# One decoder layer on one core: weight slices on GpSimd, a ring of four PSUM banks, stores waited for a stage later

## The chip, the cores and the metric

The kernel runs on one NeuronCore of a Trainium2 chip, as one program of several stages. The metric is the device time in microseconds (us) of one launch, as the median of several runs. The core has a matmul engine (TensorE, PE in the profile), a vector engine (VectorE, DVE), a scalar engine (ScalarE, ACT), GpSimd (POOL) and SyncE (SP), which only issues DMAs. The engines run apart from each other and meet at semaphores, and at a barrier at the end of every stage.

## The reference, cut to what matters

One layer of a decoder works on 1,024 prompt tokens and on 8 sequences of 4 new tokens each, width 1,024, all in float32. The parts that the change touches:

```python
# after the input projection (h @ w_in) gives qa, ka, va, c_q, ckv, kpe, ga, gb
qb = rms_norm(c_q, g_q) @ w_uq                 # queries of the latent branch
k_nope = einsum('nsc,che->nshe', ckv, w_uk)    # prompt: keys and values from the latents
v      = einsum('nsc,che->nshe', ckv, w_uv)
# new tokens: attention over the cached, paged latents (1,024 past rows per sequence)
q_lat = einsum('nthe,che->nthc', q_nope, w_uk)
s = (q_lat . ckv_ext + q_pe . kpe_ext) * scale
o = (softmax(s) . ckv_ext) . w_uv
# branch A: dilated window attention; then gates, w_o, MLP and a gated embedding
```

A product of float32 matrices is made from three matmuls: each operand is split into a high and a low part, and high x high, high x low and low x high are summed.

## The kernel before, in words

`build` calls the stages in turn. Each is one `nc.Block()`: a separate instruction list for every engine, ended by a barrier of all engines. The order of the work on an engine is the order written out in its function; nothing else plans it.

**`project_natural`** (span 0 to 261 us) projects the tokens to queries, keys, values and latents in rows of tokens. Its last steps run on ScalarE: `take(s)` (L497 to L512) copies a PSUM bank to `nat` and issues two stores, to the scratch `q_d`, `k_d` or `v_d` (L505) and to an output (L512). At its end ScalarE waits until all stores have landed (L546, L547), and only then goes to the barrier.

**`project_gates`** (261 to 509 us) multiplies the activations by 16 slices ("units") of 128 columns of the gate weights, three chunks of 352 tokens each (`multiply_chunk`, L639 to L641). GpSimd splits each unit's weights into high and low (`split_weights`, L2293 and L2295), and TensorE waits for the split of unit m before its first chunk. The first two units are split in the stage before. Between chunks, `samples_at(n)` places the pieces of the cached window attention of 8 sequences. TensorE does `turn_new` after the second chunk: it transposes the new queries and keys (`q_new`, `k_new`, L814) that SyncE has loaded from the scratch. SyncE's list is in this order: the cached keys of sequence 0 into a ring (`load_keys(0)`: four DMAs of 64 KB, L1796, and one of 1 MB, L1797), `q_new` (L773), `k_new` (L774), the cached values of sequence 0 (`load_values(0)`, five such DMAs), mask, new values, `load_keys(1)`, 14 loads of latent weights (`load_latent_weights`), and then the gate weights of units 2 and 3 (`load_unit`, L758). ScalarE stores a unit's gates (L973) and at the end waits for those stores (L979).

**`project_latents`** (509 to about 600 us) runs over nine groups of up to 128 tokens. In step t TensorE transposes latents (`turn_latents`, L1093 to L1102), multiplies the queries (`queries`, L1120 to L1122) and transposes them (`turn_queries`, L1138). VectorE does `scale_latents(t+1)` (L1263), `take_keys(t+1)` (L1273, L1274, L1277), then waits for ScalarE's query copies and does `rotate_queries(t)`, six operations on SBUF (L1288 to L1295). ScalarE makes high parts and copies the queries. GpSimd makes the low parts `cq_lo` (L1067) and `ckv_lo` (L1072), clears half of `kb_t` in step 0 (L1076), and in steps 2 and 4 splits the two weight arrays `w_uk` and `w_uv` whole: L1081 (high) and L1083 (low), 128x1024 each. They are needed only after the nine steps. Before the steps VectorE does `scale_latents(0)`, the three low parts of `w_uq` (L1302) and `take_keys(0)`.

**`attend_latent`** follows, and then **`attend_latent_sample`** (759 to 824 us), the attention over the cached latents, in two batches of four sequences. For each sequence TensorE transposes eight page tiles of 2 x 128 columns in four groups, and one rotary group (`turn_keys`, L1878 and L1881). Group n goes to PSUM bank 3 + n % 2, and is copied out by ScalarE (even n, L1967) or VectorE (odd n, L1838 and L1840); group n waits for the copy of group n - 2. The order on TensorE is: keys of sequences 0 to 3, `scores(0)` (L1897 to L1909), keys 4 and 5, `turn_probs(0)` (L1919, to banks 5 and 6), keys 6, `values(0)` (L1932, L1934), keys 7, `turn_result(0)`, `scores(1)`, `turn_probs(1)`, `values(1)`, `turn_result(1)`, and the products with `w_uv`. After the scores VectorE finds the largest (L1997) and ScalarE takes the exponential (L1971), and each of them is written ahead of that engine's copies of keys 4. SyncE loads the cached rows of sequences 3 to 7 in this stage (`load_rest`, L1764), eight DMAs each.

Window attention (`attend_window`) and the tail (merge, MLP, embedding; `run_tail`) are as before.

## Time and profile before

| | |
|---|---|
| runs | 2025.71, 2026.61, 2032.1 us; median 2026.61 |
| the profiled execution's own time | 2029.21 us |
| its span | 2027.5 us |
| TensorE matmul busy | 1912.4 us, 94% |
| TensorE weight load busy | 1760.7 us, 87% |
| VectorE, ScalarE, GpSimd busy | 795.1, 498.5, 754.1 us |
| mean granted TensorE clock | 0.974 of full speed |

Times in the profile are counted from the start of the span. A row of a timeline gives the start, the time taken, the engine, the line, the operation, output<-input, shapes and count, and in brackets how long the engine had been idle before it and what ended that. PEclk 1.00 is TensorE's 2.4 GHz, 0.50 its 1.2 GHz.

### The profile page before, as it was taken

The page shows a single profiled execution, that of the slowest core. Times are in us where ns is not written, and L with a number is a line of the kernel's source. Part 1 is how long each engine was busy: PE and PEld are TensorE (multiplying, and loading weights), DVE is VectorE, ACT ScalarE, POOL GpSimd, SP SyncE. Part 2 cuts the span into 40 slices and gives each one's busy share as a digit, 9 for nine tenths or more (in the row PEclk, how much of TensorE's full clock was granted, in tenths as well). Part 3 has the DMA queues.
Part 4 walks back from the last instruction along what each step waited for, and adds up shares of the span by engine and source line. Part 5 has one row for each costly group of instructions (what it writes and reads, how often), then busy time and mean ns, then how long its engine had stood idle before and what let it go on. Part 6 is the DMA issues. An engine that isn't in the chain of part 4 may idle for free.

```text
span 2027.5 us, 35016 instructions
## 1 busy us (share of the span) xinstructions
PE 1912.4 (94%) x13421; PEld 1760.7 (87%) x13421; DVE 795.1 (39%) x1752; ACT 498.5 (25%) x1052; POOL 754.1 (37%) x519
## 2 busy tenths in 40 slices
PE   6899979999799988798999999999999999999898
PEld 6887779998666665677999999999999999999897
DVE  4244212222636663475445531123112212255565
ACT  4232112232446552363112110001001000122222
POOL 4312112321404101100666565355436534566421
PEclk9999989999799999799999999999999999999999
DMA  6333374551002005503431331232133113311202
GB/s 215 97 104 109 125 219 148 184 178 61 10 23 68 6 1 181 136 2 129 142 102 42 115 134 52 83 125 93 45 131 126 52 42 125 134 42 42 81 24 86
DMA packets 184508, 193.40 MB, mean 95 GB/s; under 512 B 16314, under 2 KB 157466, under 8 KB 183618
## 3 DMA queue, kind: packets, MB, share of 16 engines
q1 hardware_dynamic: 167138, 161.85, 24.9%
q10 hardware_dynamic: 14816, 28.12, 4.0%
q0 software_dynamic: 2432, 1.74, 0.3%
q8 instruction: 84, 1.38, 0.3%
q14 instruction: 38, 0.31, 0.0%
HBM read 161.13 MB, written 63.97 MB: 111 GB/s over the span
## 4 chain that ended last, share of the span: by engine, by line
PE 49%; DVE 1%; DMA 1%; issue 1%; ACT 1%; POOL 0%; DVEq 0%; ACTq 0%; POOLq 0%
PE bank L639 16%; PE bank L640 16%; PE bank L641 16%; DMA f_gates<-gate_d 1%; DVE x_res L2372 0%; PE bank L2439 0%; PE bank L2400 0%; DVE f_diag L2457 0%; PE bank L2402 0%; PE bank L2401 0%; DMA out_y_prompt<-y_nat 0%; PE bank L2476 0%; PE bank L2429 0%; DVE f_hg L2370 0%; ACT tail_square L2247 0%
## 5 line engine op out<-in xcount | busy, mean ns | idle before, releaser
L639 PE MATMUL bank<-h_hi,wu_hi_tail 128*128 128x352 f32 x960 | 310.9, 324 | 3.4 <-POOL wu_lo_tail L2295 3.4
L640 PE MATMUL bank<-h_lo,wu_hi_tail 128*128 128x352 f32 x960 | 308.4, 321 | 0.0
L641 PE MATMUL bank<-h_hi,wu_lo_tail 128*128 128x352 f32 x960 | 308.4, 321 | 0.0
L2293 POOL TENSOR_TENSOR wu_hi_tail<-w_stage_tail,ones 128x1024 fp32r<-128x1024 f32 x88 | 168.4, 1914 | 273.2 <-PE bank L641 161.8
L639 PE MATMUL bank<-a_hi,wu_hi_tail 128*128 128x352 f32 x768 | 247.7, 323 | 0.0
L640 PE MATMUL bank<-a_lo,wu_hi_tail 128*128 128x352 f32 x768 | 246.1, 320 | 0.0
L641 PE MATMUL bank<-a_hi,wu_lo_tail 128*128 128x352 f32 x768 | 245.9, 320 | 0.0
L2295 POOL TENSOR_TENSOR wu_lo_tail<-w_stage_tail,wu_hi_tail 128x1024 fp32r<-128x1024 f32 x88 | 219.6, 2495 | 6.9
L2250 ACT ACTIVATE a_hi<-f_hg 128x352 f32 x96 | 47.8, 498 | 603.0 <-DVE f_hg L2356 603.0
L639 PEld LDWEIGHTS bank<-h_hi,wu_hi_tail 128*128 128x128 f32 x960 | 180.6, 188 | 3.7 <-issue 3.7
L2339 DVE TENSOR_TENSOR x_res<-bank,x_res 128x352 f32 x120 | 63.0, 525 | 301.4 <-PE bank L641 301.2
L640 PEld LDWEIGHTS bank<-h_lo,wu_hi_tail 128*128 128x128 f32 x960 | 180.9, 188 | 0.0
L641 PEld LDWEIGHTS bank<-h_hi,wu_lo_tail 128*128 128x128 f32 x960 | 180.8, 188 | 0.0
L2305 POOL TENSOR_TENSOR a_lo<-f_hg,a_hi 128x352 f32 (+1 forms) x96 | 91.1, 950 | 144.9 <-ACT a_hi L2250 144.9
L640 PEld LDWEIGHTS bank<-a_lo,wu_hi_tail 128*128 128x128 f32 x768 | 144.3, 188 | 0.0
L639 PEld LDWEIGHTS bank<-a_hi,wu_hi_tail 128*128 128x128 f32 x768 | 144.1, 188 | 0.0
L641 PEld LDWEIGHTS bank<-a_hi,wu_lo_tail 128*128 128x128 f32 x768 | 143.9, 187 | 0.0
L2353 DVE TENSOR_TENSOR f_tmp<-bank,rstd_bc 128x352 f32<-128x352 f32 x96 | 50.3, 524 | 233.2 <-PE bank L641 233.0
L639 PE MATMUL bank<-h_hi,wu_hi_gates 128*128 128x352 f32 x384 | 129.3, 337 | 10.6 <-POOL wu_lo_gates L2295 6.8
L436 PE MATMUL bank<-wn_hi,h_hi 128*128 128x512 f32 (+5 forms) x360 | 133.6, 371 | 0.0
L438 PE MATMUL bank<-wn_hi,h_lo 128*128 128x512 f32 (+5 forms) x360 | 131.6, 365 | 0.0
L437 PE MATMUL bank<-wn_lo,h_hi 128*128 128x512 f32 (+5 forms) x360 | 131.2, 364 | 0.0
(332 smaller groups left out, 3759.0 us busy)
## 6 DMA issues: line engine op xcount, KB each, us to landing
w_stage_tail<-in_w_up SPq DMA_DIRECT2D x32, 512.0 KB, 4.0
w_stage_tail<-in_w_down SPq DMA_DIRECT2D x32, 512.0 KB, 3.8
gate_d<-gate_out ACTq DMA_DIRECT2D x16, 528.0 KB, 3.4
f_gates<-gate_d ACTq DMA_DIRECT2D x24, 352.0 KB, 3.2
w_stage_gates<-in_w_in SPq DMA_DIRECT2D x16, 512.0 KB, 6.8
ws_ring<-in_cache_win_k SPq DMA_DIRECT2D x8, 1024.0 KB, 5.7
ws_ring<-in_cache_win_v SPq DMA_DIRECT2D x8, 1024.0 KB, 6.6
ls_keys<-in_cache_ckv SPq DMA_DIRECT2D x64, 128.0 KB, 2.2
```

Of the source, the lines that this page charges most:

```text
L436: pe.matmul(out, a, w, start=k == 0, stop=False)
L437: pe.matmul(out, a, v, start=False, stop=False)
L438: last = pe.matmul(out, c, w, start=False, stop=k == KD - 1)
L639: pe.matmul(out, w, a, start=n == 0, stop=False)
L640: pe.matmul(out, w, b, start=False, stop=False)
L641: last = pe.matmul(out, v, a, start=False, stop=n == len(ks) - 1)
L2250: act.activation(chunk_of(st.out[0], i, q), g.hg[:, q % 2:q % 2 + 1, :], ACT.Copy).then_inc(g.hi_s, 1)
L2293: pool.tensor_tensor(g.wu_hi[:, j], g.w_stage[:, j], one, ALU.mult).then_inc(g.w_hi, 1)
L2295: pool.tensor_tensor(g.wu_lo[:, j], g.w_stage[:, j], g.wu_hi[:, j].bitcast(F32), ALU.subtract).then_inc(g.w_split, 1)
L2305: pool.tensor_tensor(chunk_of(st.out[1], i, q), g.hg[:, q % 2:q % 2 + 1, :], chunk_of(st.out[0], i, q).bitcast(F32), ALU.subtract).then_in ...
L2339: dve.tensor_tensor(x, g.bank[:, q:q + 1, :CH], x, ALU.add).then_inc(g.free, 1)
L2353: dve.tensor_tensor(g.tmp[:, q % 2, :], g.bank[:, q, :CH], g.rstd_bc[:, c * CH:(c + 1) * CH], ALU.mult).then_inc(g.free, 1)
```

## The change

Four edits, in four stages:

1. ScalarE no longer waits for the last stores at the end of `project_natural`. Those who read or overwrite what is stored wait in `project_gates`: SyncE before the loads of `q_new` and `k_new`, and ScalarE and VectorE before their first copies of turned cached keys. `load_values(0)` now stands ahead of these two loads.
2. In the same way the stores of the gates are waited for in `project_latents`: by GpSimd before its clearing of `kb_t`, and by VectorE before `take_keys(0)`, which now comes after the first of the three low parts of `w_uq`, ahead of the other two.
3. The split of `w_uk` and `w_uv` goes in eight slices of 128x256, one in each of the steps 0 to 7.
4. The cached latent attention turns into a ring of four banks (3 to 6), group n into bank 3 + n % 4, waiting for the copy of group n - 4. The probabilities' transposes take two places of the same ring (groups 30, 31 and 42, 43), and the keys of sequences 6 and 7 are numbered after them.

```diff
@@ project_natural
-            for j in range(3):
-                act.wait_ge(nat_out[j], written(len(stored), j))
@@ project_gates
+    def wait_stored(eng):
+
+        for j in range(3):
+            eng.wait_ge(g.nat_out[j], g.nat_stored[j])
+
     def take_turned(copy, eng, s, qs, odd):
...
+            if n < 2:
+                wait_stored(eng)
             eng.wait_ge(turned, n + 1)
...
             load_keys(0)
+            load_values(0)
+            wait_stored(sp)
             sp.dma_start(q_new[:, :], g.q_d[SEQ:, :]).then_inc(new_in, 16)
             sp.dma_start(k_new[:, :], g.k_d[SEQ:, :]).then_inc(new_in, 16)
-            load_values(0)
             sp.wait_ge(clear, 1)
...
-            for j in range(2):
-                act.wait_ge(gate_out[j], 16 * (units // 2))
@@ project_latents
                 if t == 0:
+                    for j in range(2):
+                        pool.wait_ge(g.gate_out[j], g.gates_stored)
                     odd_heads = g.kb_t[:RD].rearrange("p (a two) c -> p a two c", two=2)[:, :, 1, :]
                     pool.memset(odd_heads, 0.0).then_inc(clear, 1)
                     pool.wait_ge(l_in, LATENT_LOADS)
-                if t in (2, 4):
-                    hi, lo, w = ((uk_hi, uk_lo, g.w_uk_sb), (uv_hi, uv_lo, g.w_uv_sb))[t // 2 - 1]
-                    one = g.ones[:, 0:1].unsqueeze(2).to_broadcast([P, 2, H * E])
-                    pool.tensor_tensor(hi[:, :, :], w[:, :, :], one, ALU.mult).then_inc(w_hi_s, 1)
-                    pool.wait_ge(w_hi_s, t // 2)
-                    pool.tensor_tensor(lo[:, :, :], w[:, :, :], hi[:, :, :].bitcast(F32), ALU.subtract).then_inc(w_lo_s, 1)
+                if t < NT - 1:
+                    hi, lo, w = ((uk_hi, uk_lo, g.w_uk_sb), (uv_hi, uv_lo, g.w_uv_sb))[t // 4]
+                    part = (slice(None), t // 2 % 2, slice(t % 2 * 256, t % 2 * 256 + 256))
+                    pool.tensor_tensor(hi[part], w[part], g.ones[:, 0:1].to_broadcast([P, 256]), ALU.mult).then_inc(w_hi_s, 1)
+                    pool.wait_ge(w_hi_s, t + 1)
+                    pool.tensor_tensor(lo[part], w[part], hi[part].bitcast(F32), ALU.subtract).then_inc(w_lo_s, 1)
...
             scale_latents(0)
-            for k in range(3):
-                dve.wait_ge(uq_hi_s, k + 1)
-                dve.tensor_tensor(uq_lo[:, k, :], g.w_uq_sb[:, k, :], uq_hi[:, k, :].bitcast(F32), ALU.subtract).then_inc(uq_lo_s, 1)
+            low_query_weights(0)
+            for j in range(2):
+                dve.wait_ge(g.gate_out[j], g.gates_stored)
             take_keys(0)
+            low_query_weights(1)
+            low_query_weights(2)
@@ attend_latent_sample
+    base = [groups * s + (2 if s >= 6 else 0) for s in range(NSEQ)]
+    probs_at = [6 * groups, NSEQ * groups + 2]
+    ring = lambda n: 3 + n % 4
...
-                    if n >= 2:
-                        pe.wait_ge(k_got[n % 2], n // 2)
+                    if n >= 4:
+                        pe.wait_ge(k_got[n % 2], n // 2 - 1)
...
             def turn_probs(b):
                 pe.wait_ge(e_done, b + 1)
...
+                for half in range(2):
+                    n = probs_at[b] + half
+                    pe.wait_ge(k_got[n % 2], n // 2 - 1)
+                    for a in range(4):
+                        at = (4 * half + a) * P
+                        last = pe.transpose(g.bank[:, ring(n), a * P:(a + 1) * P], prob[:, at:at + P], g.ident[:, :])
+                    last.then_inc(k_full, 1)
```

## Rows read from the trace of the kernel before

**Rows 1.** PE's waits, whole span: line, releaser, us in total, times, longest us

```profile
PE bank L1138 <- DVE q_nat L1295: 7.0, 3, 2.8
```

**Rows 2.** Timeline, 250 to 272 us, the change from `project_natural` to `project_gates`

```profile
258.27 0.70 ACTq L512 DMA_DIRECT2D out_win_v_sample<-nat  x1
...
260.90 0.55 PE L639 MATMUL bank<-h_hi,wu_hi_gates 128*128 128x352 f32 x1 [3.74 <-PEq L310]
```

**Rows 3.** Lines L547 and L979: duration ns min/median/max, first and last start us

```profile
L547 ACTq EVENT_SEMAPHORE  x1: 38/38/38, 260.4 to 260.4; - x1
...
L979 ACTq EVENT_SEMAPHORE  x1: 17/17/17, 508.5 to 508.5; - x1
```

**Rows 4.** DMA issues at 262.62, 263.09 and 265.96 us: count, KB, us to landing

```profile
ws_ring<-in_cache_win_k SPq DMA_DIRECT2D x1, 1024.0 KB, 5.7
...
ws_q_new<-q_d SPq DMA_DIRECT2D x1, 64.0 KB, 5.2
...
ws_ring<-in_cache_win_v SPq DMA_DIRECT2D x1, 1024.0 KB, 8.6
```

**Rows 5.** Timeline, 268 to 300 us, up to the first wait for split weights

```profile
270.37 0.43 PE L814 MATMUL bank<-ident,ws_q_new 32*128 32x32 f32 x4
...
291.19 1.89 POOL L2293 TENSOR_TENSOR wu_hi_gates<-w_stage_gates,ones 128x1024 fp32r<-128x1024 f32 x1 [28.80 <-DMA w_stage_gates<-in_w_in]
...
295.56 0.66 PE L639 MATMUL bank<-h_hi,wu_hi_gates 128*128 128x352 f32 x1 [6.83 <-POOL wu_lo_gates L2295]
```

**Rows 6.** Table by stretches: length, busy by engine, then PEclk, DMA share, GB/s

```profile
298.00:299.00 1.00, 1.00 (x6) 1.00 (x6) 0.00 (x0) 0.00 (x0) 1.00 (x1) 0.73 0.77 229
```

**Rows 7.** Timeline, 505 to 515 us, the change from `project_gates` to `project_latents`

```profile
505.83 0.34 ACTq L973 DMA_DIRECT2D gate_d<-gate_out  x1
...
509.36 0.87 PE L1093 MATMUL bank<-ident,cq 128*128 128x128 f32 x3 [4.54 <-PEq L751]
...
512.22 2.08 DVE L1302 TENSOR_TENSOR uq_lo<-w_uq_sb,uq_hi 128x768 fp32r<-128x768 f32 x2 [0.46 <-ACT uq_hi L1199]
```

**Rows 8.** Timelines of DVE and POOL in `project_latents`, 538 to 554 us

```profile
538.82 0.55 DVE L1263 TENSOR_TENSOR cq_x<-bank,g_q_sb 128x384 f32<-128x384 f32 x1
...
542.96 1.53 DVE L1288 TENSOR_TENSOR lat_ra<-q_nat,cos_b_sb 128x128 f32<-128x128 f32 x1 [1.73 <-ACT q_nat L1244]
...
544.62 2.43 DVE L1290 TENSOR_TENSOR lat_rb<-q_nat,sin_b_sb 128x128 f32<-128x128 f32 x1
...
547.82 0.55 DVE L1263 TENSOR_TENSOR cq_x<-bank,g_q_sb 128x384 f32<-128x384 f32 x1
...
553.42 0.55 DVE L1263 TENSOR_TENSOR cq_x<-bank,g_q_sb 128x384 f32<-128x384 f32 x1
...
541.75 0.74 POOL L1072 TENSOR_TENSOR ckv_lo<-ckv_t,ckv_hi 128x256 fp32r<-128x256 f32 x1 [0.74 <-ACT ckv_hi L1212]
542.45 1.90 POOL L1081 TENSOR_TENSOR uv_hi<-w_uv_sb,ones 128x1024 fp32r<-128x1024 f32 x1
544.42 2.48 POOL L1083 TENSOR_TENSOR uv_lo<-w_uv_sb,uv_hi 128x1024 fp32r<-128x1024 f32 x1
```

**Rows 9.** Timeline of `attend_latent_sample`, 759 to 824 us

```profile
763.90 1.06 PE L1878 MATMUL bank<-ident,ls_keys 128*128 128x128 f32 x8 [0.50 <-DVE ls_key_t L1838]
...
780.36 1.23 DVE L1997 CUSTOM_DVE_ANT_0 ls_prob<-bank,ls_mask 128x1028 f32<-128x1028 f32 x1 [5.94 <-PE bank L1909]
...
783.41 1.97 PE L1878 MATMUL bank<-ident,ls_keys 128*128 128x128 f32 x8 [2.21 <-ACT ls_key_t L1967]
...
794.42 3.66 PE L1932 MATMUL bank<-ls_keys,ls_prob_t 128*32 128x256 f32 x64
...
802.52 1.92 PE L1897 MATMUL bank<-ls_key_t,ql_t 128*32 128x512 f32 x16 [0.34 <-issue]
```

**Rows 10.** Line L1764, issues of 759.0 to 763.7 us: count, duration ns, starts

```profile
L1764 SPq DMA_DIRECT2D ls_keys<-in_cache_ckv x9: 332/333/347, 759.4 to 763.6; - x9
...
DMA to landing us min/median/max: 2.0/2.3/5.4
```

More of the change, by code:

```diff
@@ L292, in project_natural @@
         g.sem, ("wn_in", "wn_hi", "wn_lo", "n_full", "n_got", "roped", "tabs", "ra_s"))
-    nat_out = [g.sem(f"nat_out{j}") for j in range(3)]
+    nat_out = g.nat_out = [g.sem(f"nat_out{j}") for j in range(3)]
     g.w_stage = Room(nc, g.gate_stage_at)("w_stage_gates", [P, 2, KD, P])
@@ L303, in written @@
         return 16 * sum(1 if stored[n][0] == 2 else 2 for n in range(place, m, 3))
+    g.nat_stored = [written(len(stored), j) for j in range(3)]
     def low_block(eng, b):
@@ L713, in project_gates @@
     gate_ready = g.sem("gt_ready")
-    gate_out = [g.sem(f"gt_out{j}") for j in range(2)]
+    gate_out = g.gate_out = [g.sem(f"gt_out{j}") for j in range(2)]
     ring_in = [sem(f"ring_in{j}") for j in range(3)]
@@ L1831, in take_keys @@
         for q in range(groups):
-            n = s * groups + q
+            n = base[s] + q
             if n % 2 != odd:
@@ L1840, in take_keys, with take_probs @@
                 copy(rope_t[:, s % BATCH, :, :].rearrange("p a c -> p (a c)"), src[:, :2 * P]).then_inc(k_got[odd], 1)
+    def take_probs(copy, eng, b, odd):
+        half = (odd - probs_at[b]) % 2
+        n = probs_at[b] + half
+        eng.wait_ge(k_full, n + 1)
+        if b >= 1:
+            eng.wait_ge(o_full, b)
+        copy(prob_t[:, 4 * half:4 * half + 4, :].rearrange("p a b -> p (a b)"), g.bank[:, ring(n), :]).then_inc(k_got[odd], 1)
     with nc.Block() as block:
@@ L1866, in turn_keys @@
                 for q in range(groups):
-                    n = s * groups + q
+                    n = base[s] + q
                     if q == 0:
@@ L1957, in _ @@
             pe.wait_ge(ot_got, 2)
+            for odd in range(2):
+                pe.wait_ge(k_got[odd], done(probs_at[1] + 2, odd))
             for h in range(H):
@@ L1984, in _ @@
             take_keys(copy, act, 5, 0)
-            take_probs(0)
+            take_probs(copy, act, 0, 0)
             take_keys(copy, act, 6, 0)
@@ L1988, in _ @@
             exponent(1)
-            take_probs(1)
+            take_probs(copy, act, 1, 0)
         @block.vector
```

57 lines of the change are left out of this document (25 added, 32 removed).

## The prediction

> **What bounds the kernel now.** The table of the profile says that TensorE is busy for 94% of the span, so time can only come from its idle stretches and from stretches at its lower clock. I read its waits first, then the timelines around the places that the change touches. The longest wait inside a stage is for the rotated queries [rows 1]. Three more places matter.
>
> At the first stage change TensorE is idle for 3.74 us up to 260.90 [rows 2]. ScalarE's last issue ends at 258.97 [rows 2], its wait for that store ends at 260.44 [rows 3], and 0.46 us later the next stage runs. At the second change the last issue ends at 506.17 [rows 7], the wait at 508.5 [rows 3], and the stage starts at 509.36 after 4.54 us of idling [rows 7]: 0.84 us after the wait.
>
> In `project_latents` VectorE sets the pace. From one L1263 to the next it takes 5.60 us without a weight split (547.82 to 553.42) and 9.00 us with one (538.82 to 547.82) [rows 8]. The 3.40 us are two rotations: L1288 lasts 1.53 us and ends 0.14 us after GpSimd's high part, L1290 lasts 2.43 us and ends 0.15 us after the low part [rows 8]. L1289 between them is not held.
>
> In the cached latent attention TensorE transposes two groups (eight transposes, 1.06 us) and then waits for a copy (0.50 us [rows 9], elsewhere down to 0.35): some 1.44 us for two groups. Without the waits, and as the last transpose's tail lies beside the next, it would be 0.92, or 0.46 us a group. After the scores both copying engines are taken by the softmax, TensorE runs dry for 2.21 us until 783.41, and then eight transposes take 1.97 us [rows 9]: the 1.2 GHz level.
>
> **The change, part by part.**
>
> *First stores waited later: 2.7 us.* The next stage starts 0.46 us after 258.97, at 259.43, so 1.47 us earlier. But `q_new` and `k_new` now stand behind the cached values. Before, the queries were issued at 263.09 and landed 5.2 us later [rows 4], at the very time at which the megabyte of keys ahead of them landed (262.62 + 5.7), and the megabyte of values landed 8.6 us after 265.96 [rows 4], 13.7 us into the stage. So this queue's data come one after the other, and the two small loads will land 12.5 to 13.7 us into the stage; I take 13.2, that is 272.6. TensorE needs them 9.5 us in (270.37 [rows 5]): a new stall of about 4 us, after which it stands 2.3 us later than before, and at the lower clock for a time, which costs another 1 to 2.5 us. What is late next is nothing: TensorE used to arrive at the third unit at 288.73 and to wait 6.83 us for its split [rows 5]. It now arrives 18.4 us after 272.6 plus the clock, at 292 to 293.5. The split hangs on SyncE's issues, whose order from the mask on is the same, and its data, GpSimd's 28.80 us of idling ending with them [rows 5]; it is ready 1.47 us earlier, at about 294.1. Cover for the stall is gone if the arrival goes beyond that. With the wait shrunk from 6.8 to about 1 us the clock should stay up: after 295.56 it was at 1.2 GHz until about 298.5 (0.73 in the slice from 298 [rows 6]), half of 3.0 us lost; I count 1.2 of these 1.5. Sum 1.47 + 1.2 = 2.7; bounds -0.5 (arrival past the split) and 3.2. SyncE's own wait costs nothing: it comes 4.5 us into the stage, the stores land 1.0 us into it. The waits of ScalarE and VectorE come after the fourth chunk, later still. `load_values(1)`, which waits for transposes before the third unit, is issued about 3.5 us later, but its values are used over 25 us after that.
>
> *Gate stores waited later: 2.3 us.* The stage starts 0.84 us after 506.17, at 507.0 instead of 509.36. VectorE comes to its new wait about 2.4 us in, at 509.4, GpSimd 5.4 us in, after the 508.5 at which the stores had landed: no cost. Bounds 2.0 and 2.7 (the 0.46 us of the first change).
>
> *Start of the latents: 1.2 us.* `take_keys(0)` moves ahead of two low parts (2.08 us for both [rows 7]), and TensorE's step 1 and the first queries with it: 2.2 us. GpSimd gives back 1.0: its first slice stands ahead of `cq_lo` of step 1, so that `cq_lo`, `ckv_lo` and the second slice all fall on the first rotation. Bounds 0 and 2.2.
>
> *Slices: 4.5 us.* A 128x256 subtraction takes 0.74 us, a 128x1024 one 2.48 [rows 8]: 0.58 us per 256 columns and 0.16 fixed. The 1.90 us of the high part [rows 8] give 0.16 + 1.74 / 4 = 0.60. In a step's time, with 542.45 as the start: high part to 543.05, low part 543.12 to 543.86. VectorE comes with L1288 at 542.96, as before, is held for 0.1 us (hidden by its own latency), passes L1289, and L1290 ends at 543.86 + 0.15 = 544.01 instead of 543.65: 0.37 us a step. Six steps (2 to 7) cost 2.2 us in place of 2 x 3.40 = 6.8: 4.6, say 4.5. Bounds: no hold at all (6.8), and a hold for the whole of both slices, 1.34 us a step (-1.2). I take the working by the rows since it follows the order seen there. The weights' last slice ends in step 7, before the products that need them.
>
> The Trainium skill, SBUF — State Buffer, "Who interferes with whom", says that VectorE with two SBUF inputs and GpSimd exclude each other for a whole instruction and that the one issued first has the port. The row agrees (2.43 us beside a 2.48 us one). Taken at its worst, a rotation held by every slice, the slices would cost more than the two whole arrays; that is a rival below.
>
> *Ring of four: 10.2 us.* The first stretch runs at 1.2 GHz until 763 and is TensorE's own; no gain. From then on a sequence (four groups and a half) takes 2.1 us instead of 3.3. Sequences 1 and 2 end at 767.5. SyncE issues nine loads of pages from 759.4 to 763.6, so sequence 3's eighth at 763.0, and the longest of them takes 5.4 us to land [rows 10]: 768.5, one us of waiting. The scores start at 771.2 instead of 774.5: 3.3 us. From there to L1997 (780.36) and to the copy that released 783.41 [rows 9] nothing changes: 3.05 us. But TensorE has four groups to do in it instead of two, idles for 1.4 us instead of 2.2, and has only rotary 4, sequence 5, the probabilities (together 3.3), sequence 6 (2.1), `values(0)` (3.66 [rows 9], with its small end 4.2), sequence 7 (2.1) and 0.8 of result and last copy left, all at full clock: 12.5 us. So `scores(1)` follows 3.05 + 12.5 = 15.5 us, say 15.3, after L1997 starts; before it was 802.52 - 780.36 = 22.2 [rows 9]: 6.9 us. Together 10.2. Nothing changes behind it. Bounds: 6.8 if the clock falls in the 1.4 us wait as it did before (from 783.2 to 790 at half rate, 3.4 us), and 13.4 if it stays up after the second softmax, too.
>
> **Sum**: 2.7 + 2.3 + 1.2 + 4.5 + 10.2 = 20.9 us. The profiled execution took 2029.2 (span 2027.5 and 1.7 around it), so 2008.3; it stands 2.6 us above the median of the runs, which gives 2005.7, and I predict 2006 for the median.
>
> **The rivals** (times as medians).
> - *The clock falls in the softmax wait.* For it: a 2.21 us gap was followed by 1.97 us for eight transposes [rows 9]. Against it: the gap is now 1.4 us with work on both sides. 17.5 us, 2009. Chance 0.20. The mirror case, one stretch of low clock less elsewhere, gives 2002.5: 0.10.
> - *The late queries are not absorbed.* They land beyond 14 us or the clock stays low for longer, so that TensorE reaches the third unit after its split. The first term falls to -0.5: 2009. Chance 0.10; the wait of 6.83 [rows 5] speaks against it.
> - *The slices hold the rotations for their full length.* 1.34 x 6 = 8.0 in place of 6.8: the slices' term is -1.2, in sum 15.2, 2011.5. L1289, which passed between two GpSimd operations [rows 8], speaks against it. Chance 0.07. It is what the skill's rule on the shared port gives at its worst.
> - *The ring doesn't run ahead*, because pages arrive late: at the pace of [rows 10] the 40 loads are issued by 781 and landed by 784; the last sequence is needed at 790. Only sequence 3 should wait; if each of the later ones waits 1 us, 2010. Chance 0.02.
> - *Slower than before.* In the ring the bursts and pauses of TensorE leave the clock at 1.2 GHz over the whole cached stage. It has some 44 us of work at full rate; each us of it at half rate costs one. It decides once 27 us more of this work than I count are at the lower level: all 44 would give 2029 to 2040. Against it: with the pauses of the old order the level was 2.4 GHz for most of the stage. Chance 0.02.
>
> **How the numbers follow.** My forecast has the remaining 0.49. Its own range, from clock alignment and the unknown port order, is 2002 to 2010. With the rivals the range is 2000 to 2015. A measurement here can tell 0.3% (6 us) from no change: faster by more than that 0.95 (all cases but the slow one and a pile-up of two or three of the others), within it 0.03, slower 0.02.
>
> **What would show it.** First gate stage: L814 waits for DMA about 4 us, then the wait for L2295 is about 1 us instead of 6.8. The second stage starts near 259.4, the third 1.2 us after the start of the last store's issue. L1263 to L1263 near 6.0 us in steps 2 to 7, no more 9.0, L1288 and L1290 under 1 us. In the cached stage no wait for key copies except at the softmax (about 1.4 us), scores 11.9 us after the stage's start (before 15.2), and eight transposes near 1.0 us afterwards. It is wrong if L1263's period is above 6.6, if TensorE is ready after the third unit's split, or if the cached stage is shortened by less than 7 us.

## The result, and the profile after

The changed kernel takes 2012.42 us, the median of four runs (2007.71 to 2014.73), beside 2028.15 for the kernel before on the same chip: a ratio of 0.991, with a 95% interval of 0.9894 to 0.9925 (the ratios here are estimated from all the runs; the two medians alone would give 0.992). The forecast was 2006, in a range of 2000 to 2015. So the sign and the range held, and about a quarter of the 20.9 us I had summed up did not come: the profiled executions are 2029.2 us before and 2013.7 after, 15.5 us apart.

I followed the gain from place to place. Each number is the start of the same instruction before less its start after:

| place | before | after | gained so far |
|---|---|---|---|
| first gate product | 260.90 | 259.60 | 1.30 |
| first transpose of the latents | 509.36 | 505.47 | 3.89 |
| third scaling of the latents | 524.21 | 519.30 | 4.91 |
| ninth scaling | 564.63 | 556.37 | 8.26 |
| first key product behind them | 573.69 | 565.27 | 8.42 |
| first transpose of the cached stage | 759.33 | 752.25 | 7.08 |
| its first scores | 774.53 | 766.50 | 8.03 |
| its second scores | 802.52 | 787.57 | 14.95 |
| first transpose of the next stage | 824.16 | 809.85 | 14.31 |

TensorE's timeline of the kernel after, in the gates' stage (start us, duration, engine and line; in brackets the idle time before it and what ended it), and under it GpSimd's:

```profile
259.60 0.40 PE L639 MATMUL bank<-h_hi,wu_hi_gates 128*128 128x352 f32 x1 [2.60 <-PEq L312]
...
273.78 0.63 PE L822 MATMUL bank<-ident,ws_q_new 32*128 32x32 f32 x4 [4.75 <-DMA ws_k_new<-k_d]
...
295.42 0.43 PE L639 MATMUL bank<-h_hi,wu_hi_gates 128*128 128x352 f32 x1 [1.49 <-POOL wu_lo_gates L2318]
...
291.04 1.90 POOL L2316 TENSOR_TENSOR wu_hi_gates<-w_stage_gates,ones 128x1024 fp32r<-128x1024 f32 x1 [29.95 <-DMA w_stage_gates<-in_w_in]
```

The reader is to see that the wait of 6.83 us for the split [rows 5] has become two: 4.75 us for the new keys, which TensorE takes up at 273.78 where the forecast had them landed at 272.6, and 1.49 us for the split. But TensorE goes on at 295.42 where it went on at 295.56 before: the third unit's weights arrive at 291.0 as before [rows 5], although the stage began 1.3 us earlier. ("Arrive" is the start of GpSimd's split, which ends its wait for them.) The table by stretches (length, busy time of PE, PEld, DVE, ACT and POOL, granted clock as a share of 2.4 GHz, DMA share, GB/s) shows what the second wait was worth. Of the kernel after:

```profile
270.00:275.00 5.00, 1.22 (x9) 1.16 (x10) 0.12 (x1) 0.13 (x1) 0.00 (x0) 0.61 1.04 263
275.00:280.00 5.00, 5.00 (x24) 5.00 (x25) 0.75 (x3) 0.00 (x0) 0.00 (x0) 0.71 0.75 176
...
295.00:300.00 5.00, 4.58 (x32) 4.06 (x36) 0.85 (x2) 0.60 (x1) 4.61 (x3) 1.00 0.90 282
```

and of the kernel before:

```profile
295.00:300.00 5.00, 4.44 (x19) 4.45 (x20) 0.00 (x0) 0.00 (x0) 4.73 (x3) 0.65 0.62 184
```

Before, TensorE came out of the wait at the lower level and ran 19 of the recorded products up to 300; now it comes out at 2.4 GHz and runs 32. The low clock has moved into the stretches from 270 to 280 (0.61 and 0.71), where the time it costs would have been waited away at 293.9 in any case.

In the latents, VectorE's and GpSimd's timelines of one step after:

```profile
519.30 0.55 DVE L1276 TENSOR_TENSOR cq_x<-bank,g_q_sb 128x384 f32<-128x384 f32 x1
...
523.44 0.29 DVE L1301 TENSOR_TENSOR lat_ra<-q_nat,cos_b_sb 128x128 f32<-128x128 f32 x1 [1.73 <-ACT q_nat L1253]
523.65 0.87 DVE L1302 TENSOR_TENSOR lat_ra<-q_nat,cos_b_sb 128x128 f32<-128x128 f32 x1
524.44 0.28 DVE L1303 TENSOR_TENSOR lat_rb<-q_nat,sin_b_sb 128x128 f32<-128x128 f32 x1
...
525.49 0.55 DVE L1276 TENSOR_TENSOR cq_x<-bank,g_q_sb 128x384 f32<-128x384 f32 x1
...
522.93 0.62 POOL L1090 TENSOR_TENSOR uk_hi<-w_uk_sb,ones 128x256 fp32r<-128x256 f32 x1
523.63 0.74 POOL L1092 TENSOR_TENSOR uk_lo<-w_uk_sb,uk_hi 128x256 fp32r<-128x256 f32 x1
```

The steps of 9.00 us are gone [rows 8]; each of the steps from the third scaling to the ninth takes 6.15 to 6.19 us now. One operation of a rotation, L1302, is held: it ends at 524.52, 0.15 us after GpSimd's low part, as the held ones did before. In one step it went the other way:

```profile
536.02 0.29 DVE L1302 TENSOR_TENSOR lat_ra<-q_nat,cos_b_sb 128x128 f32<-128x128 f32 x1
536.22 0.83 DVE L1303 TENSOR_TENSOR lat_rb<-q_nat,sin_b_sb 128x128 f32<-128x128 f32 x1
...
536.00 0.90 POOL L1092 TENSOR_TENSOR uv_lo<-w_uv_sb,uv_hi 128x256 fp32r<-128x256 f32 x1
```

Here L1302 keeps its 0.29 us, GpSimd's low part takes 0.90 us in place of 0.74, and L1303 is the one held.

The cached stage after:

```profile
752.25 3.57 PE L1906 MATMUL bank<-ident,ls_keys 128*128 128x128 f32 x16 [1.21 <-PEq L1366]
...
757.88 1.91 PE L1906 MATMUL bank<-ident,ls_keys 128*128 128x128 f32 x16
...
762.18 3.32 PE L1906 MATMUL bank<-ident,ls_keys 128*128 128x128 f32 x16 [2.18 <-DMA ls_keys<-in_cache_ckv]
...
766.50 1.92 PE L1924 MATMUL bank<-ls_key_t,ql_t 128*32 128x512 f32 x16 [0.56 <-ACT ls_key_t L1997]
...
775.38 0.44 PE L1909 MATMUL bank<-ident,ls_rope 128*128 128x128 f32 x2 [1.33 <-ACT ls_key_t L1997]
...
787.57 1.92 PE L1924 MATMUL bank<-ls_key_t,ql_t 128*32 128x512 f32 x16 [0.34 <-ACT ls_key_t L1997]
...
772.33 1.23 DVE L2021 CUSTOM_DVE_ANT_0 ls_prob<-bank,ls_mask 128x1028 f32<-128x1028 f32 x1 [5.94 <-PE bank L1936]
```

Sixteen transposes (four groups) in one run of 1.91 us where pairs of groups used to take 1.06 us and then wait [rows 9]: the four banks keep TensorE free of the copies. What it meets instead is sequence 3's pages, for 2.18 us, and behind that wait sixteen transposes take 3.32 us: the granted clock was 0.50 from 763 to 766.

### The profile page after: what moved, and what is told of

The parts are those of the page before. It is cut to its first block, busy times and chain, and to the rows that moved or that the text cites. A ratio compares the mean times of both kernels' runs of the same rounds, so it can differ in the third digit from the quotient of the medians.

```text
span 2012.0 us, 35033 instructions
## 1 busy us (share of the span) xinstructions
PE 1907.1 (95%) x13421; PEld 1757.5 (87%) x13421; DVE 793.5 (39%) x1752; ACT 498.6 (25%) x1052; POOL 758.1 (38%) x531
## 4 chain that ended last, share of the span: by engine, by line
PE 51%; DMA 1%; DVE 1%; POOL 0%; issue 0%; ACT 0%; DVEq 0%; POOLq 0%; ACTq 0%
PE bank L639 16%; PE bank L640 16%; PE bank L641 16%; DMA f_gates<-gate_d 1%; PE bank L2423 0%; PE bank L2424 0%; PE bank L2425 0%; DMA out_y_prompt<-y_nat 0%; PE bank L2462 0%; DVE f_diag L2480 0%; PE bank L2452 0%; PE bank L2499 0%; POOL wu_lo_tail L2318 0%; ACT y_nat L2298 0%; POOL a_lo L2328 0%
## 5 line engine op out<-in xcount | busy, mean ns | idle before, releaser
L2316 POOL TENSOR_TENSOR wu_hi_tail<-w_stage_tail,ones 128x1024 fp32r<-128x1024 f32 x88 | 169.8, 1930 | 272.6 <-PE bank L641 161.8
```

The source lines that it names most:

```text
L2316: pool.tensor_tensor(g.wu_hi[:, j], g.w_stage[:, j], one, ALU.mult).then_inc(g.w_hi, 1)
```

## The experiments

Ten kernels answered the questions below, and an eleventh joins the edits that helped; each is the changed kernel with the edit shown. The times are medians with the ratio to the kernel before, measured beside it (before: 2028.2 to 2029.8 us). There is one profiled execution of each kernel, and stages whose text an experiment leaves alone show how far one execution differs from the next. From the first gate product to the first scaling of the latents the changed kernel and experiments 4 to 9 have the same text and took 245.1 to 246.8 us (246.49 in the changed kernel). The cached stage has the same text in the changed kernel and in experiments 1, 2, 3, 7, 8 and 9, and took 54.0 to 57.6 us. A difference inside these spreads is not shown by one pair of traces. I read the stages more than the totals; the intervals of the totals overlap that of the changed kernel in experiments 1 to 4, 7 and 9.

**1. The third and fourth units' loads ahead** (2011.07 us, 0.9907, 0.9872 to 0.9942).

```diff
+            load_unit(2)
+            load_unit(3)
             load_keys(1)
             load_latent_weights(g, sp)
```

(and no more in the loop's first round). The text below says ten loads of latent weights; there are fourteen.

> The changed kernel, with the loads of the third and fourth gate unit issued ahead of the second sequence's window keys and the latent weights instead of behind them. Theory: the head start of the first stores was lost because these two loads stand on SP behind ten loads of latent weights, which back up in the DMA queue. Then both units land before 280 us (in the changed kernel 290.9 and 292.4), GpSimd has split them before TensorE comes for them, TensorE's wait of 1.49 us for the split is gone, the wait of 4.75 us for the new keys stays, and the whole falls by 1.5 us (1 to 2.5) against the changed kernel. Rival: what holds these loads is the traffic itself, not their order; then they take their time from the keys and queries around them, and nothing is gained, or up to 2 us lost.

```profile
272.95 0.63 PE L824 MATMUL bank<-ident,ws_q_new 32*128 32x32 f32 x4 [3.58 <-DMA ws_k_new<-k_d]
...
280.12 1.89 POOL L2318 TENSOR_TENSOR wu_hi_gates<-w_stage_gates,ones 128x1024 fp32r<-128x1024 f32 x1 [18.70 <-PE bank L641]
```

GpSimd now waits for TensorE to free the buffer (280.12), no longer for the load, and TensorE has no wait for a split left. From the first gate product to the first scaling of the latents it takes 244.35 us, against 246.49: 2.1 us less, and 0.75 less than the shortest execution with the old order. The split hung on the place of these loads in SP's list: they are issued from 268.3 instead of 283.5, and land some 7.5 us after their issue in both kernels. That no wait for the split is left does not show it by itself: experiments 4, 8 and 9 have none either, with the old order. The total shows 1.35 us of it.

**2. The queries ahead of the values** (2013.87 us, 0.9913, 0.9881 to 0.9946).

```diff
             load_keys(0)
-            load_values(0)
             wait_stored(sp)
             sp.dma_start(q_new[:, :], g.q_d[SEQ:, :]).then_inc(new_in, 16)
             sp.dma_start(k_new[:, :], g.k_d[SEQ:, :]).then_inc(new_in, 16)
+            load_values(0)
```

> The changed kernel, with the new queries and keys of the window stage loaded ahead of the first sequence's window values, behind the same wait for the stores. Theory: TensorE's 4.75 us for the new keys is hidden behind the wait for the third unit's split. Then the new keys land near 269 us instead of 273.7, the wait of 4.75 us falls under 1 us, the wait for the split grows from 1.49 to between 5.5 and 6.5 us, TensorE restarts at 295.4 as before, and the whole is the same within 1 us (apart from the clock, which may stay up and give up to 1 us). Rival: the wait is on the path, and the whole falls by over 4 us.

```profile
268.44 0.43 PE L822 MATMUL bank<-ident,ws_q_new 32*128 32x32 f32 x4 [1.48 <-DMA ws_k_new<-k_d]
294.26 0.66 PE L639 MATMUL bank<-h_hi,wu_hi_gates 128*128 128x352 f32 x1 [7.43 <-POOL wu_lo_gates L2318]
...
295.00:300.00 5.00, 5.00 (x22) 5.00 (x22) 0.00 (x0) 0.00 (x0) 3.42 (x2) 0.63 0.44 109
```

The last line is this kernel's stretch from 295 in the table. The early wait shrank by 3.3 us, not to under 1 as expected, and the one for the split grew to 7.43, beyond the 5.5 to 6.5; TensorE comes out of it at the low clock again, and the gates' stage takes 248.02 us to the first scaling, 1.5 more than the changed kernel's and 1.2 more than the longest execution with its text. The total is 1.45 us above it, where I had expected the same within 1 us. The 4.75 us were hidden, and the wait in two halves is even better than one: the low clock behind the first half is hidden, too.

**3. The first boundary as it was before** (2014.09 us, 0.9933, 0.9917 to 0.9949): ScalarE waits for the stores at the end of `project_natural`, the later waits for them are gone, and the queries are loaded ahead of the values.

```diff
+            for j in range(3):
+                act.wait_ge(nat_out[j], written(len(stored), j))
...
-            wait_stored(sp)
```

> The changed kernel with the first boundary as it was before: ScalarE waits for the stores at the end of the projection stage, and SP loads the new queries and keys ahead of the window values. Theory: the earlier start of 1.3 us is worth nothing by itself, since the third unit's weights land no earlier with it; what the change gained there is that TensorE's wait is split, so that the half clock behind it falls into time in which TensorE would have waited anyway. Then TensorE waits for the split 6.8 us here and runs at half the clock behind it, and from the first gate matrix product to the first scaling of the latents it takes 247.1 us as before (less the 2.36 us of the second boundary) against 246.5; the whole loses 1.3 to 2.5 us. Rival: the start is worth its 1.3 us, and another 1.5 are the clock's; the loss is 2.7 us or more.

```profile
260.85 0.63 PE L641 MATMUL bank<-h_hi,wu_hi_gates 128*128 128x352 f32 x1 [3.73 <-PEq L312]
295.55 0.66 PE L641 MATMUL bank<-h_hi,wu_hi_gates 128*128 128x352 f32 x1 [6.11 <-POOL wu_lo_gates L2317]
...
290.00:295.00 5.00, 0.00 (x0) 0.00 (x0) 0.00 (x0) 0.69 (x2) 3.74 (x2) 0.83 0.93 284
295.00:300.00 5.00, 4.45 (x15) 4.46 (x16) 0.00 (x0) 0.00 (x0) 4.71 (x3) 0.50 0.73 224
```

TensorE starts 1.25 us later and goes on at 295.55, 0.13 us after the changed kernel's 295.42. From there to the first scaling it takes 212.73 us, against 210.67: the 2.06 us lie behind the wait, where the clock is at half. This pair is more than chance: from the same restart experiment 2, at half clock too, took 212.73, and experiments 5, 6 and 7, which waited 0.4 to 1.5 us and kept the clock, took 210.66 to 210.72. The first scaling comes 2.19 us later and the total is 1.7 us longer, as the theory had it; the stage by itself (247.43) is 0.3 us above its figure. Of the head start of 1.25 us 0.13 is left at the restart (0.4 to 1.1 in experiments 5, 6 and 7, whose stages began a little earlier); the clock is worth two microseconds.

**4. GpSimd's masks behind the fourth sequence's pages** (2008.02 us, 0.9897, 0.9858 to 0.9936).

```diff
+            pool.wait_ge(ahead.k_in[ahead.early], 16 * NPAGE)
             for j in range(BATCH):
                 pool.dma_start(mask[rows(j), :], g.mask_ls_c).then_inc(mask_in, 16)
```

> The changed kernel, with GpSimd's four mask loads and its load of new values in the cached stage held back until the fourth sequence's pages have landed. Theory: the ring gained only 1 us at the first scores because these pages landed 10 us after the stage's start, behind GpSimd's loads, and the clock fell in the wait. Then the pages land by about 7.5 to 8.5 us, TensorE waits for them under 1 us, keeps its clock, and begins the first scores 10.5 to 11.2 us after the stage's start (14.25 in the changed kernel), and the whole falls by 3 to 3.7 us against the changed kernel. Rival 1: the eleven DMAs ahead of TensorE are slow for their own sake (pages of 128 KB each, one every 0.52 us); the landing moves by under 0.5 us and nothing else does. Rival 2: the masks come late in their place, VectorE's first maximum waits for them, and the stage ends no earlier.

```profile
749.66 1.94 PE L1907 MATMUL bank<-ident,ls_keys 128*128 128x128 f32 x16 [1.21 <-PEq L1366]
...
756.70 1.97 PE L1907 MATMUL bank<-ident,ls_keys 128*128 128x128 f32 x16 [0.95 <-DMA ls_keys<-in_cache_ckv]
...
759.45 1.92 PE L1925 MATMUL bank<-ls_key_t,ql_t 128*32 128x512 f32 x16 [0.56 <-ACT ls_key_t L1998]
```

The pages land 7.0 us after the stage's start instead of 9.9, TensorE waits 0.95 us for them, and sixteen transposes behind the wait take 1.97 us, not 3.32. The first scores begin 9.79 us after the start (14.25): 4.5 us less. The distance to the second scores is 21.07 us in both, so the masks are not missed. The median is 4.4 us lower, the forecast was 3 to 3.7. How much of it is the edit, the other executions tell (us after the stage's start; "goes on" is where the sixteen transposes of the fourth sequence start):

| masks | experiment | TensorE goes on | its wait for the pages | first scores | whole stage |
|---|---|---|---|---|---|
| early | changed kernel | 9.93 | 2.18 | 14.25 | 57.60 |
| early | 1 | 9.31 | 1.56 | 12.06 | 54.70 |
| early | 2 | 9.60 | 3.52 | 13.82 | 57.10 |
| early | 3 | 8.84 | 1.14 | 11.59 | 54.35 |
| early | 7 | 10.36 | 4.27 | 14.61 | 57.43 |
| early | 8 | 8.47 | 0.72 | 11.22 | 54.04 |
| early | 9 | 10.24 | 4.16 | 14.57 | 57.39 |
| held | 4 | 7.04 | 0.95 | 9.79 | 51.24 |
| held | 10 | - | none | 10.28 | 53.59 |
| held | 11 | 7.92 | 0.18 | 10.67 | 53.98 |

With the early masks the stage falls into two kinds: after waits of 2.18 us and more the sixteen transposes ran at half the clock, after 1.56 us and less they did not, and the two kinds are 3 us apart. With the masks held no execution is of the long kind. The means of the stage are 56.1 and 52.9 us, so the edit is worth some 3 us there, and the 51.24 of this execution is the best of its kind: experiments 10 and 11 began the stage at half the clock and needed 0.5 and 0.9 us more to the first scores. What makes the pages land at 8.5 us in one execution and at 10.4 in another is not shown. The Trainium skill, DMA: Bandwidth & Descriptors, "Queues, rings and completion order", says that each DMA engine takes its queues in turn, a packet from each; the landing, 2.9 us earlier once GpSimd's queue was quiet (and earlier in experiments 10 and 11 than in any execution with early masks), agrees with it.

**5. Two banks in the cached stage** (2020.79 us, 0.9952, 0.9936 to 0.9969), and **6. two banks with the masks behind the pages** (2018.77 us, 0.9949, 0.9934 to 0.9965): `attend_latent_sample` with the old function's text, in the second with the edit of 4 as well.

```diff
-    ring = lambda n: 3 + n % 4
...
-                    if n >= 4:
-                        pe.wait_ge(k_got[n % 2], n // 2 - 1)
+                    if n >= 2:
+                        pe.wait_ge(k_got[n % 2], n // 2)
```

> The changed kernel with the cached stage as it was before: two banks in turn for the keys, banks of their own for the probabilities. What the ring is worth by itself: the cached stage, from its first transpose to the first transpose of the next stage, takes 64.8 us again instead of 57.6, so the whole is 7.2 us longer (6 to 8.5, the clock within the stage included). Rival: a part of the 7.2 us comes from elsewhere (the stage's start, the clock it starts with), and the loss is under 5 us.

> The changed kernel with two banks in the cached stage and with GpSimd's masks held behind the fourth sequence's pages. Theory: with two banks TensorE, held by the copies, reaches the fourth sequence only after its pages have landed in any case, so the loads' order is worth nothing: the first scores begin 15.2 us after the stage's start, as with two banks and the old order, and the whole is the same as that kernel within 1 us. It is the ring that puts the loads on the path. Rival: the order of the loads helps by itself, and the first scores come earlier than 14.5 us.

TensorE before the first scores, with two banks, and with two banks and the late masks:

```profile
766.39 0.44 PE L1896 MATMUL bank<-ident,ls_rope 128*128 128x128 f32 x2 [0.35 <-DVE ls_key_t L1853]
767.39 1.92 PE L1912 MATMUL bank<-ls_key_t,ql_t 128*32 128x512 f32 x16 [0.56 <-issue]
```

```profile
765.86 0.44 PE L1897 MATMUL bank<-ident,ls_rope 128*128 128x128 f32 x2 [0.35 <-DVE ls_key_t L1853]
766.86 1.92 PE L1913 MATMUL bank<-ls_key_t,ql_t 128*32 128x512 f32 x16 [0.56 <-issue]
```

The stages began at 752.17 and 751.65, so the first scores came 15.22 and 15.21 us later: the order of the loads is worth nothing while the copies hold TensorE. The whole stage took 64.92 and 64.86 us, against 57.60: the ring is worth 7.3 us against this execution of it, 10.2 to 10.8 against those that kept the clock (54.0 to 54.7, table in 4), and 10.9 to 13.6 with the masks held (54.0 to 51.2). The medians of the runs are 8.4 and 6.4 us above the changed kernel's. The two medians differ by 2.0 us where I had allowed 1; the stages are equal to 0.1.

**7. The weight parts as whole arrays again** (2013.37 us, 0.9929, 0.9912 to 0.9946).

```diff
-                if t < NT - 1:
+                if t in (2, 4):
...
-                    part = (slice(None), t // 2 % 2, slice(t % 2 * 256, t % 2 * 256 + 256))
```

> The changed kernel with the weight parts taken as whole arrays again, in the third and the fifth step. From the second to the last scaling of the latents it takes 40.4 us (37.1 in the changed kernel), 3.3 us more. If the 1.2 us that the changed kernel lost behind this stretch (its first key products at half the clock) come from the slices, then these products run at full clock here and the whole loses only 2 us; if they come from chance, the low clock shows in some runs of either kind, and the whole loses 3.3 us.

Between the third scaling and the ninth it takes 40.48 us, against 37.07: 3.4 us. But from the first scaling to the third it takes 12.02 us, against 13.21: the first two slices cost 1.2 us there. So the slices are worth 2.2 us in all, and the median is only 1.0 higher. The total of the rival, 3.3 us more, left this out. The first six key products take 2.28 us here, partly at the low clock as in the changed kernel (2.70; 1.45 in the kernel before), so that loss is no work of the slices.

**8. The slices early, with a wrong tie** (2043.53 us, 1.0066, 1.0045 to 1.0086), and **9. with the right one** (2007.2 us, 0.9889, 0.9872 to 0.9905).

```diff
+                if t >= 1:
+                    pool.wait_ge(qr, t)
+                    split_part(t - 1)
                 pool.wait_ge(cq_hi_s, t + 1)
```

and in 9:

```diff
+                if t >= 1:
+                    if t >= 2:
+                        pool.wait_ge(qr, t - 1)
+                    split_part(t - 1)
                 pool.wait_ge(cq_hi_s, t + 1)
```

`split_part` is the slice's two operations, taken out of the end of the step.

> The changed kernel, with each slice of the weight parts taken at the start of the next step, as soon as VectorE has finished a rotation, so that it lies beside VectorE's reads of PSUM and not beside the rotation. Theory: of a slice only the low part costs, since it holds one instruction of the rotation to 0.87 us instead of 0.29. Then all six instructions of a rotation take 0.28 to 0.30 us, a step falls from 6.19 to 5.6 or 5.7 us, and the whole by 3.5 to 4 us against the changed kernel. Rival 1: the low latents start 0.26 us later behind the slice and that is on the loop; a step takes 5.85 and the whole falls by 2.3 us. Rival 2: GpSimd holds VectorE's reads of PSUM just as well (0.69 and 0.68 us become 0.9 and more), and the step stays at 6.2 us.

> The changed kernel, with each slice taken right after the rotation of two tiles before, one step earlier than in the last try, where the slice had tied a tile's low latents to the rotation of the tile before it and laid the steps end to end (9.8 us each). In that run GpSimd's slices beside VectorE's reads of PSUM lengthened neither, and no rotation was held. Theory: without the tie the six instructions of a rotation take 0.28 to 0.30 us each, the low latents start 0.4 us later, which has slack, a step takes 5.6 to 5.7 us (6.19 in the changed kernel), and from the second to the last scaling it saves 3.4 to 4 us. Rival: the 0.4 us are on the loop, and a step takes 6.0 us or more.

VectorE and GpSimd in one step of kernel 9:

```profile
522.00 0.29 DVE L1306 TENSOR_TENSOR lat_ra<-q_nat,cos_b_sb 128x128 f32<-128x128 f32 x1 [1.73 <-ACT q_nat L1258]
522.21 0.28 DVE L1307 TENSOR_TENSOR lat_ra<-q_nat,cos_b_sb 128x128 f32<-128x128 f32 x1
522.41 0.28 DVE L1308 TENSOR_TENSOR lat_rb<-q_nat,sin_b_sb 128x128 f32<-128x128 f32 x1
...
523.47 0.55 DVE L1281 TENSOR_TENSOR cq_x<-bank,g_q_sb 128x384 f32<-128x384 f32 x1
524.05 0.69 DVE L1291 COPY kb_t<-bank 32x512 f32<-32x512 f32 x1
...
529.07 0.55 DVE L1281 TENSOR_TENSOR cq_x<-bank,g_q_sb 128x384 f32<-128x384 f32 x1
...
523.63 0.61 POOL L1071 TENSOR_TENSOR uk_hi<-w_uk_sb,ones 128x256 fp32r<-128x256 f32 x1 [2.10 <-DVE q_nat L1313]
524.33 0.73 POOL L1073 TENSOR_TENSOR uk_lo<-w_uk_sb,uk_hi 128x256 fp32r<-128x256 f32 x1
```

Kernel 8 was my mistake: its wait made a tile's low latents follow the rotation of the tile before, VectorE then sat idle for 5.9 us a step, and a step took 9.8 us. Even so it showed that nothing is held when a slice lies beside reads of PSUM. Kernel 9 waits one rotation less: no rotation is held, the reads of PSUM beside the slices take their 0.69 and 0.68 us, a step takes 5.60 us, and from the third to the ninth scaling it takes 33.62 us, 3.45 less than the changed kernel. The median is 5.2 us lower. Its last slice stands ahead of the last low latents, for which TensorE waits 0.55 us: from the ninth scaling to the key products it takes 10.04 us, 8.90 in the changed kernel. The other half microsecond I did not follow. The Trainium skill, SBUF — State Buffer, "Who interferes with whom", says that a VectorE operation with two SBUF inputs contends with a GpSimd operation that reads SBUF, one with at most one such input (here) does not, and that the one issued first has the port for its whole length. The rows agree on the first two points: in the changed kernel L1302 was held to the low part's end, here L1291 beside a slice was not. The third they bear out in that one of the two always kept its length; which one, the start times do not tell at 0.02 us apart, since at 536.00 and 536.02 it was the one recorded second.

**10. The edits of experiments 1, 2 and 4 together** (2003.13 us, 0.9875, 0.9858 to 0.9891).

> The changed kernel with three edits together: the third and fourth units' loads ahead, the new queries ahead of the window values, GpSimd's masks behind the fourth sequence's pages. By itself the first took about 2.1 us off the gates' stage, where its one wait left is that for the new keys (3.6 us); the second cut that wait from 4.75 to 1.48 us, but the wait for the split took it over. Theory: together both waits go, the gates' stage is another 2 us shorter, and the third edit saves 3 to 4.5 us in the cached stage. The whole falls by 7 to 8.5 us against the changed kernel. Rival: the new keys and the units' weights share the queue, and each delays the other; then the gates' stage gains only 2 us, and the whole 5 to 6.

The gates' stage takes 237.59 us to the first scaling, 8.9 less than the changed kernel's, and 4 to 5 more than I had counted on: of TensorE's waits inside the stage (4.75 and 1.49) 0.8 us is left, and the granted clock is 1.00 over 255 to 300. In the changed kernel it averaged 0.89 there, with three stretches of 5 us at 0.61 to 0.71, the first of them (260 to 265) behind the start of the stage, which no edit touches. An estimate from these rows: 5.4 us of waits, and half of the 7.5 us that TensorE worked at the lower level (3.4 behind the start, 4.1 behind the keys), 9.2 in all. The total falls by 9.3 us, more than the 7 to 8.5 expected. The row of this kernel:

```profile
255.00:300.00 45.00, 41.59 (x281) 38.95 (x283) 9.58 (x19) 11.33 (x19) 10.17 (x7) 1.00 0.82 237
```

**11. The edits of 1, 2, 4 and 9 together, the last slice behind the last low latents** (1995.89 us, five runs of 1994.63 to 1999.25, 0.9844, 0.983 to 0.9859).

> The changed kernel with the four edits that helped: the units' loads ahead, the queries ahead of the window values, the masks behind the fourth sequence's pages, and the slices one step earlier (the last of them behind the last low latents, which it had delayed). If the parts add, the gates' stage takes 237.6 us to the first scaling (246.5 in the changed kernel), the scalings from the second to the last 33.6 us (37.1), the cached stage 51 to 54 us (57.6), and the whole comes to 1997 to 2001 us in the middle of its runs, 1.5% under the kernel before. Rival: the clock takes some back at the seams between the stages, and it comes to 2002 or more.

TensorE's chief rows, and GpSimd's first split:

```profile
738.09 3.59 PE L1916 MATMUL bank<-ident,ls_keys 128*128 128x128 f32 x16 [1.21 <-PEq L1375]
...
746.01 1.97 PE L1916 MATMUL bank<-ident,ls_keys 128*128 128x128 f32 x16 [0.18 <-DMA ls_keys<-in_cache_ckv]
...
274.54 1.90 POOL L2326 TENSOR_TENSOR wu_hi_gates<-w_stage_gates,ones 128x1024 fp32r<-128x1024 f32 x1 [13.99 <-DMA w_stage_gates<-in_w_in]
```

To the first scaling 238.3 us, from the third to the ninth 33.6, the cached stage 54.0: the parts add. It is 16.5 us faster than the changed kernel, a microsecond beyond the 1997 to 2001 expected, and the fastest of all.

## Why the prediction was right or wrong

- **Sign and place: right.** Every stage gained where the steps said; behind the cached stage, where nothing was changed, 1.2 us more came by chance. The chance of 0.95 for faster stands.
- **First stores, 2.7 us: 1.5 to 2.2 in this execution, and in part for another reason.** The step that failed is that the split "is ready 1.47 us earlier, at about 294.1": it was ready at 295.37, 0.13 us earlier than before. SyncE's issues stand in the same order, but behind the latent weights the third unit's was only 0.7 us earlier (283.54, before 284.23), and its weights landed at 291 as before. Counted from the first gate product the split was ready 0.3 to 1.5 us later than before in six of the seven executions with this stage's text, so most often a part of the head start is lost. The part "the clock should stay up" carried the gain here. It is 1.5 us at the end of the gates' stage against the kernel before, and 2.2 us at the first scaling against experiment 3, where I had counted 1.2 for it. With the spread of the other executions it is 1.7 to 3.5 us, so the 2.7 is not refuted as a size. The stall of "about 4 us" measured 4.75, as the keys came 1.2 us later than the 272.6 forecast, and was absorbed (experiment 2). In experiments 4, 8 and 9 TensorE even came after the split, which the forecast names as a sign of being wrong, yet the stage took no longer than in the others.
- **Gate stores, 2.3 us: right.** 3.89 us at the start of the latents, less the 1.5 that TensorE already had when it finished the gates (the last operation of VectorE there ended that much earlier), is 2.4.
- **Start of the latents, 1.2 us: near, in part by luck.** 1.02. Of it 0.36 us lie ahead of the first scaling and were not in the sum: after an idle stretch of 2.17 us in place of 4.54 the first three transposes take 0.52 us, not 0.87. From the first scaling to the third 0.66 us are left: the earlier `take_keys(0)` gives 1.85 (13.87 before, 12.02 in experiment 7), where I had 2.2, and the first slices take back 1.2, where I had 1.0.
- **Slices, 4.5 us: mis-sized, 3.35.** The failed step is "passes L1289". By my own times that operation comes 0.2 us behind 542.96, at 543.16, and the low part starts at 543.12, ahead of it. So it is the second operation that meets the low part and is held to its end, with two more products to come behind it instead of one. A rotation is 1.52 us from L1301 to L1306 instead of 0.93: 0.59 us a step, not 0.37, so a step of 6.19 us, not 5.97. In one step (536.22) the third operation was the held one, as I had it, and it still took 6.15 us.
- **Not in my sum: 1.25 us behind the latents.** The first key products ran at half the clock after (0.63 us each) and at full clock before (0.39). Of the eleven experiments' profiled executions four ran them at full clock (1, 4, 8 and 11) and seven lower for a part, with slices and with whole arrays: I take it for chance at this seam. That the kernel before is always at full clock here was not tried, with one trace of it.
- **Ring, 10.2 us: 7.2 in this execution, 7.3 to 10.8 over the seven with its text** (experiment 5 and the table in 4). The failed step is "one us of waiting" for sequence 3, with nothing behind it. Counted from the stage's start the forecast had TensorE ready at 8.2 us and the pages landed at 9.2; measured are 7.8 and 9.9. The wait was 2.18 us, and the half clock behind it, which the sum put at nothing, cost another 1.4 (3.32 us for sixteen transposes against 1.91). The first scores came 14.25 us into the stage, not 11.9. In experiments 1, 3 and 8 the pages landed 8.5 to 9.3 us after the start, the wait was 0.7 to 1.6 us, the clock stayed up, and the stage was 10.2 to 10.8 us shorter than with two banks: there the forecast holds. So the term was the better of two cases that the trace before could not tell apart. The second half was right: from the first maximum to the second scores 15.24 us, forecast 15.3; the wait at the softmax 1.33 us, forecast 1.4, and the clock stayed up. Another 0.6 us were lost behind the second scores, where executions differ by as much (21.6 to 22.3 us to the next stage with early masks).
- **The rivals.** "The clock falls in the softmax wait" did not happen: it fell in the wait for the pages, one stall earlier. "The slices hold the rotations for their full length" did not: one operation in six is held, and takes 0.87 us instead of 0.28. "The late queries are not absorbed" did not cost anything, as said above. The rival of late pages had the right place and at 0.02 far too small a chance, though only sequence 3 was late, not the later ones. The slower rival did not come near: by the stretches of its table some 17 of the cached stage's 58 us were at the lower level, and it needed 27 us of TensorE's work there more than I had counted. Its bracket of 2029 to 2040 for all 44 us does not follow from its own rule, since 27 us more than counted are already 2033.
- **A reading.** "The longest wait inside a stage is for the rotated queries" is not what the view shows. The query that gives [rows 1] has two larger sums, the first of them with a single wait of 9.1 us:

```profile
PE bank L418 <- DVE x_t L570: 9.8, 2, 9.1
```

Nothing in the sum hangs on it.

By place the 15.5 us are 3.9 at the two boundaries, 1.0 at the start of the latents, 3.35 by the slices, 0.2 and then -1.35 between the last scaling and the cached stage, 7.2 in it, and 1.2 in the long last part, which the change doesn't touch. The shortfall of 5.4 us against my sum is 3 in the ring, 1.2 in the slices, 1.2 in the first boundary and 1.25 at the key products, less those 1.2.

## What to carry to other kernels

When an edit takes away what held an engine, the next limit was hidden in its shadow and is not in the old trace as a wait: list the landing time of every input of the faster stretch beside the time at which its engine will now ask for it. Where the two are within a microsecond or two, put the half clock behind the wait into the sum as a case of its own: it cost 1.4 us beside a wait of 2.18 here, and it came in four executions of seven. Look at a queue's order before its speed: two loads moved past fourteen that nobody needs for 200 us, two more ahead of some values, and four masks and one small load held back, brought 9.3 us, more than half as much as the whole change. A wait that cannot be avoided is best placed ahead of another one that has slack, since the half clock behind it is then free (2 us in experiments 2 and 3). One profiled execution of each kernel does not size a gain of a few microseconds; the stages that an experiment leaves alone give the spread for nothing.

## What the runs showed of the hardware that was not expected

TensorE's clock behind a wait decides as much as the wait. After 6.1 to 7.4 us of waiting for the split it ran at 0.50 to 0.65 of 2.4 GHz over 295 to 300, some 2 us lost; after 0.4 to 1.5 us it did not fall at all. In the cached stage it fell after 2.18, 3.52, 4.16 and 4.27 us of waiting for the pages, and not after 0.18, 0.72, 0.95, 1.14 and 1.56 us. But the same seam falls either way. Behind the 2.6 us of idling at the start of the gates' stage the clock stayed at 1.00 in experiment 10 and fell in experiment 11 (mean 0.96 over 255 to 300), with the same text. The cached stage's first sixteen transposes took 3.4 to 3.6 us in six executions with the ring and 1.94 us in four, with much the same work ahead of them.
